# A transformer kernel on one core: input splits, square sums, a transfer and a modulation moved in the order of the engines

## The chip, the cores and the metric

The kernel runs on one core of a Trainium2 chip. The metric is the device time of one execution in microseconds (us); a lower time is better. Three runs of the kernel before took 2363.65 to 2364.48 us, with a median of 2364.28.

## The reference

All arithmetic is float32. There are 256 tokens of width 1024 and a second input, a context of 256 tokens. The first block has two layers: RMS norm, input projection, four kinds of attention, output projection, RMS norm, and a squared-ReLU network.

```python
        x = x + mixed @ w_out[layer]
        h2 = _rmsnorm(x, norm_mlp[layer])
        x = x + jnp.square(jax.nn.relu(h2 @ w_up[layer])) @ w_down[layer]
    return _rmsnorm(x, final_norm)
```

The second block works on tokens and context. Its first mixer is an mLSTM with four heads: queries and keys, a gated and decayed product of them, values, an output gate and an RMS norm of each head. Its last lines:

```python
        o = jax.nn.sigmoid(h_in @ w_og).reshape(Bq, T, M_HEADS, M_DV)
        hsum = o * s.transpose(0, 2, 1, 3).astype(h_in.dtype)
        return _head_rms_norm(hsum, norm_g) @ w_out
```

A convolved feed-forward network, a latent attention and a second feed-forward network follow.

## The kernel before, in words

Every activation lies in SBUF with features on the partitions: `xT` (the residual), `hT` (the modulated input of the second block) and an arena with everything else, reused by stage. A linear layer is a **group** of the stream plan: `("up", l, i)`, `("down", l)`, `("m_qk", h)`, `("m_og", h)` and so on. Its weights come from DRAM in slots of 128 x 2048 (1 MB) into `ring`, which has two places. It runs over **chunks** of 128 input features; `g.q0` is a group's first chunk and `g.s0` its first weight slot in the order of the whole program.

TensorE multiplies in the fp32r format with each operand split into a high and a low part, so each product is three matmuls (L757 where the activations move, L762 where the weights move). The high part is a copy made by ScalarE: `ws` from `ring` (L1236) and `xs` from the source (L1258 with a gain, L1260 without). The low part is the difference, made by VectorE (L1694, L1716, L1719). `ws` has room for two slots. `xs` has four cells of 256 columns: four chunks of 256 tokens, or two of 512. A copy waits until the chunk that held its place before has been multiplied.

ScalarE and VectorE each have the same three helpers: `weights_to(s)` splits slots up to s; `feed_to(q)` splits chunks up to q, and at the second and the last chunk of a slot also the next weight slot; `feed(g, more)` goes to the end of a group and `more` chunks beyond. Nothing is scheduled at run time: the order of each engine is the order of these calls and of the evictions between them, and an engine stands at each wait.

SyncE issues all large transfers. `load(w)` waits until the slot w - 1 has been split, then loads slot w. At the start the bias vectors (12 rows) are written to DRAM and read back as overlapping rows (`hankel`, `tz`), which VectorE reverses into the bias tables after `dma_bias`.

The results of TensorE go to eight PSUM banks, given out in a fixed order of tickets (`ticket_plan`): ticket n uses bank n % 8, so a product waits until the eviction of the ticket eight before it. In a mixer head the tickets are: 2 for the running maximum (`m_max`), 4 for `m_qk`, 4 for the scores (`m_QK`), 4 for the output gate (`m_og`), 1 for the denominator, 2 for its reciprocal, 4 for the product with the values (`m_PV`), 1 for the head's square sum (`m_rms`). The second quarter of `m_PV` so reuses the first bank of `m_og`, and chunk 0 of the next `m_qk` those of the last reciprocal and of `m_PV`.

**A mixer head.** TensorE: `m_max`, four chunks of `m_qk`, the square sum of the head before (L1089), the other twelve chunks, the scores (L1098), the output gate's eight chunks with denominator (L1109) and reciprocal (L1119) between them, then `m_PV` (L1127). ScalarE feeds `m_og` and chunk 0 of the next `m_qk`, evicts the gate by four sigmoids (L1516), loads the exp/ln table, and squares the head's 128 x 2048 result (L1519). VectorE multiplies the decays by the reciprocals (L2104), adds the two directions (L2109), feeds the gate's last chunk and chunk 0 of the next head, and multiplies `m_PV` by the gate (L2115). GpSimd adds the four squared tiles in two steps (L1672, L1674) for the first three heads; the fourth head's are summed by TensorE. At the next head VectorE continues with chunk 1, two memsets and chunks 2 and 3, then the exponents (L2060, L2067).

**Up and down.** Each up group's four bank pairs are evicted by VectorE (L1935, ReLU and scale) and squared by ScalarE (L1428) into `act`, the input of down. `relu` has two places, so the third eviction waits for the first square. At the last up group both engines first feed two chunks beyond it.

**The end of layer 1.** VectorE modulates the context half of `hT` (L1965, eight tiles), adds down's result to the residual (L1734), ScalarE squares (L1270), TensorE sums them in two steps (`group_sums` L867, `spread_sum` L877) with products of constants between them (`keep_warm`, L830) that nobody reads. ScalarE makes the root (L1294, L1296), and VectorE scales, modulates and feeds the first chunks of `m_up`.

## Time and profile before

| | us |
|---|---|
| median of 3 runs | 2364.28 |
| profiled execution, whole | 2365.65 |
| its span, first to last instruction | 2363.5 |
| TensorE busy with matmuls | 2255.5 (95%) |
| VectorE busy | 1354.2 (57%) |
| ScalarE busy | 1194.4 (51%) |
| GpSimd busy | 12.2 (1%) |

The mean granted clock of TensorE over the span is 0.995 of full speed. The span holds all stages in one stream, so a stage is read from its own stretch: layer 0 up to about 400 us, layer 1 to 774, the widening layer and the gates to 897, the values to 1082, the four mixer heads to 1460, then the rest. In a timeline row the first number is the start and the second the time from the first to the last instruction of the row; x4 is their count; in brackets stands how long the engine was idle before the row, and who released it. PE is TensorE, DVE VectorE, ACT ScalarE, POOL GpSimd, SPq the queue of SyncE.

### The profile page before, as it was taken

Reading aid. Unit: us, or ns where it says so; the run is one execution under the profiler, and the core shown is the slowest. Engines: PE = TensorE matmul, PEld = TensorE weight load, DVE = VectorE, ACT = ScalarE, POOL = GpSimd, SP = SyncE. Lnnn points to the kernel's source line nnn. Section 1 sums busy time; section 2 is a strip of 40 time slices with the busy share of each in tenths; the row PEclk is TensorE's granted clock in tenths of the full one; section 3 lists DMA queues with packets and bytes.
Section 4 is the critical chain, followed back from the end, with each engine's and each line's share of the span. In section 5 each row is a group of like instructions: output and inputs, shape, how many; then the busy total and the mean of one; then the engine's idle time right before and its main releaser. Section 6 shows DMA issues by size and latency. Waiting matters only on the chain.

```text
span 2363.5 us, 33820 instructions
## 1 busy us (share of the span) xinstructions
PE 2255.5 (95%) x13592; PEld 1859.8 (79%) x13592; DVE 1354.2 (57%) x2252; ACT 1194.4 (51%) x2020; POOL 12.2 (1%) x10
## 2 busy tenths in 40 slices
PE   8999999999999899999999999999999997899998
PEld 7759999957999777787676666867777876658998
DVE  5665655666665665445556555356565346446774
ACT  4556545555554563444344342256565335546764
POOL 0000000000000000000000000000000000000000
PEclk9999999999999999999999999999999999999999
DMA  7864544793445213222121121222222222204542
GB/s 296 324 251 143 183 174 179 281 361 125 175 165 185 85 69 107 89 89 90 53 89 54 72 72 47 96 72 89 90 89 98 99 89 73 106 19 156 184 163 106
DMA packets 45721, 312.31 MB, mean 132 GB/s; under 512 B 4951, under 2 KB 7255, under 8 KB 8580
## 3 DMA queue, kind: packets, MB, share of 16 engines
q1 hardware_dynamic: 45572, 310.20, 36.3%
q8 instruction: 108, 1.77, 0.3%
q14 instruction: 41, 0.34, 0.0%
HBM read 309.11 MB, written 1.07 MB: 131 GB/s over the span
## 4 chain that ended last, share of the span: by engine, by line
PE 80%; DVE 10%; ACT 7%; issue 2%; DMA 1%; ACTq 0%; SPq 0%; DVEq 0%
PE bank L757 56%; PE bank L762 8%; DVE ws L1694 3%; ACT ws L1236 2%; PE bank L966 2%; PE bank L1127 2%; DVE xs L1719 2%; PE bank L1027 1%; PE bank L1098 1%; PE bank L830 1%; PE bank L952 1%; PE bank L951 1%; PE bank L1008 1%; DVE arena L2104 1%; ACT xs L1260 1%
## 5 line engine op out<-in xcount | busy, mean ns | idle before, releaser
L757 PE MATMUL bank<-xs,ws 128*128 128x256 f32 (+1 forms) x9648 | 1570.0, 324 | 60.7 <-DVE xs L1719 48.9
L757 PEld LDWEIGHTS bank<-xs,ws 128*128 128x128 f32 x9648 | 1398.4, 191 | 234.0 <-DVE xs L1719 65.5
L1694 DVE TENSOR_TENSOR ws<-ring,ws 128x1024 fp32r<-128x1024 f32 x464 | 550.9, 1228 | 278.6 <-ACT ws L1236 278.4
L1236 ACT ACTIVATE ws<-ring 128x1024 fp32r<-128x1024 f32 x464 | 464.6, 1049 | 287.0 <-PE bank L757 279.2
L1719 DVE TENSOR_TENSOR xs<-arena,xs 128x512 fp32r<-128x512 f32 (+1 forms) x286 | 166.8, 599 | 305.6 <-ACT xs L1260 304.7
L1260 ACT ACTIVATE xs<-arena 128x512 fp32r<-128x512 f32 (+1 forms) x286 | 148.9, 538 | 338.1 <-PE bank L757 224.6
L762 PE MATMUL bank<-ws,xs 128*128 128x512 f32 (+1 forms) x1008 | 230.2, 388 | 6.3 <-ACT arena L1495 2.2
L1719 DVE TENSOR_TENSOR xs<-hT,xs 128x512 fp32r<-128x512 f32 (+1 forms) x216 | 133.0, 619 | 178.5 <-ACT xs L1260 178.5
L762 PEld LDWEIGHTS bank<-ws,xs 128*128 128x128 f32 x1008 | 188.5, 189 | 46.8 <-DVE xs L1719 3.2
L1260 ACT ACTIVATE xs<-hT 128x512 fp32r<-128x512 f32 (+1 forms) x216 | 122.8, 575 | 199.0 <-PE bank L757 190.3
L1716 DVE SCALAR_TENSOR_TENSOR xs<-xT,par,xs 128x256 fp32r<-128x256 f32 x112 | 51.1, 479 | 14.5 <-ACT xs L1258 11.9
L1258 ACT ACTIVATE xs<-xT,par 128x256 fp32r<-128x256 f32 x112 | 51.8, 495 | 6.8 <-DVE xT L1734 6.8
L830 PE MATMUL bank<-con 128*128 128x256 f32 x204 | 50.2, 401 | 2.2 <-DVE arena L2217 2.2
L966 PE MATMUL bank<-arena,cs 128*32 128x256 f32 x768 | 51.4, 385 | 0.0
L830 PEld LDWEIGHTS bank<-con 128*128 128x128 f32 x204 | 40.8, 202 | 11.7 <-issue 6.0
L1270 ACT ACTIVATE arena<-xT 128x512 f32<-128x512 f32 (+1 forms) x52 | 28.4, 563 | 39.5 <-DVE xT L2143 26.4
L1449 ACT ACTIVATE arena<-bank,par 128x512 f32<-128x512 f32 (+1 forms) x60 | 41.8, 697 | 11.1 <-PE bank L757 11.1
L1868 DVE SCALAR_TENSOR_TENSOR arena<-bank,arena 128x384 f32<-128x384 f32 x40 | 22.3, 557 | 41.2 <-PE bank L952 41.2
L1375 ACT ACTIVATE arena<-arena 128x128 f32<-128x128 f32 x40 | 16.1, 402 | 58.4 <-DVE arena L1871 58.4
L1127 PE MATMUL bank<-arena 128*128 128x512 f32 (+1 forms) x128 | 41.9, 485 | 0.0
L1957 DVE SCALAR_TENSOR_TENSOR arena<-arena,par 128x510 f32<-128x510 f32 (+1 forms) x60 | 38.8, 647 | 3.3 <-ACT arena L1466 3.3
L1959 DVE SCALAR_TENSOR_TENSOR arena<-arena,par 128x510 f32<-128x510 f32 (+1 forms) x60 | 39.2, 653 | 2.1
(263 smaller groups left out, 1479.0 us busy)
## 6 DMA issues: line engine op xcount, KB each, us to landing
ring<-in_stream SPq DMA_DIRECT2D x233, 1024.0 KB, 4.8
arena<-in_side SPq DMA_DIRECT2D x56, 1024.0 KB, 7.0
arena<-bias_vectors SPq DMA_DIRECT2D x1, 1536.0 KB, 10.4
hT<-in_tokens SPq DMA_DIRECT2D x1, 1024.0 KB, 6.3
arena<-in_tokens SPq DMA_DIRECT2D x1, 1024.0 KB, 13.5
out<-arena SPq DMA_DIRECT2D x2, 512.0 KB, 3.1
arena<-in_params SPq DMA_DIRECT2D x1, 918.0 KB, 9.7
arena<-bias_vectors SPq DMA_DIRECT2D x1, 706.0 KB, 11.8
```

The lines of the kernel that those rows point to most:

```text
L757: ins = mm(ps(n, c, c + g.T), a[wi][:, p * P:(p + 1) * P], x[xi], start=first, stop=last)
L762: ins = mm(ps(n, 0, width), x[xi][:, (p // nh) * P:(p // nh + 1) * P], a[wi][:, (p % nh) * 512:(p % nh) * 512 + width], start=first, stop= ...
L830: mm(ps(n, at, at + cols), ones, con[:, 0:cols], start=True, stop=True)
L966: ins = mm(bank[n % BANKS][c:c + 32, 0:T], cs[:, k, 2 * ADA_B - 2 - 2 * u:2 * ADA_B + 30 - 2 * u], wd[:, k, :], start=(u == 0 and k < 4), ...
L1127: ins = mm(ps(n, T_AT[st_], T2), mv[:, st_, h * T2 + e * P:h * T2 + (e + 1) * P], mP[:, 0, OFF[st_]:OFF[st_] + T2 - T_AT[st_]], start=(st_ ...
L1236: do(ws[:, i % 2, 0, c], ring[:, w % R, c], ACT.Copy).then_inc(w_high, 1)
L1258: do(split_x(q, 0), source(g, k), ACT.Identity, scale=par_at(g.gain, k)).then_inc(x_high, 1)
L1260: do(split_x(q, 0), source(g, k), ACT.Copy).then_inc(x_high, 1)
L1449: return do(dst, ps(n, 0, cols), ACT.Identity, scale=w[:, 1:2], bias=b)
L1694: ins = v.tensor_tensor(ws[:, i % 2, 1, c], ring[:, w % R, c], ws[:, i % 2, 0, c].bitcast(F32), ALU.subtract)
L1716: stt(split_x(q, 1), source(g, k), par_at(g.gain, k), split_x(q, 0).bitcast(F32), ALU.mult, ALU.subtract).then_inc(x_done, 1)
L1719: v.tensor_tensor(split_x(q, 1), source(g, k), split_x(q, 0).bitcast(F32), ALU.subtract).then_inc(x_done, 1)
```

## The change

Seven edits in the order of the engines; the arithmetic is the same except for the engine that adds the squares.

- Bias rows: SyncE issues the two reads of the bias vectors behind three ring loads, not four.
- Last root: three more constant products before the last `group_sums`; the eight context modulations stand between the chunk splits of layer 1's down, at chunks 10 to 17, not behind them.
- Last up group, in both layers: ScalarE and VectorE feed one chunk beyond it, not two. ScalarE splits down's chunk 1 and the weight slot behind it after two of the four squares, VectorE after the four evictions.
- Head loop, output gate: VectorE splits the gate's last chunk before the add of the two directions.
- Head loop, next head: both engines split chunks 0 and 1 of the next `m_qk` before the evictions of the gate (ScalarE) and of `m_PV` (VectorE). The weight slot behind them, which chunk 1 used to bring with it, comes after the sigmoids on ScalarE and after the first product on VectorE (`ahead=False`).
- Squares: GpSimd's two adds move to VectorE, behind the two memsets; its block goes.
- `mod_at` and `modulate_part` are defined earlier.

```diff
@@ -667,12 +667,13 @@
             sp.wait_ge(bank_free[N("bias") % BANKS], N("bias") // BANKS + 1)
             sp.dma_start(scratch, relu[0:12, 0, :]).then_inc(dma_bv, 16)
-            for i in range(4):
+            for i in range(3):
                 load(R + i)
             sp.wait_ge(dma_bv, 16)
             hnd = scratch.tensor
             sp.dma_start(hankel, bass.AP(tensor=hnd, offset=128, ap=[[1, P], [512, 12], [1, T]])).then_inc(dma_bias, 16)
             sp.dma_start(tz, bass.AP(tensor=hnd, offset=4 * 512, ap=[[1, P], [512, 4], [1, 353]])).then_inc(dma_bias, 16)
+            load(R + 3)
@@ -1044,6 +1045,7 @@
                     linear(G("up", l, i))
                 linear(G("down", l))
+            keep_warm(N(("m_up", 0)), T, T, 3)
             group_sums(2 * DEPTH)
@@ -1236,7 +1238,7 @@
                     fed["w"] += 1
-            def feed_to(q_):
+            def feed_to(q_, ahead=True):
@@ -1259,7 +1261,7 @@
                         do(split_x(q, 0), source(g, k), ACT.Copy).then_inc(x_high, 1)
                     fed["q"] += 1
-                    if (k % g.kc == 1 or k == g.K - 1) and follows(s_):
+                    if ahead and (k % g.kc == 1 or k == g.K - 1) and follows(s_):
                         weights_to(s_ + 1)
@@ -1421,8 +1423,10 @@
                 for i in range(4):
                     g = G("up", l, i)
-                    feed(g, 1 if i < 3 else 2)
+                    feed(g, 1)
                     for j in range(4):
+                        if i == 3 and j == 2:
+                            feed_to(G("down", l).q0 + 1)
                         n = N(g.name) + j
@@ -1509,11 +1513,15 @@
                     act_.wait_ge(bank_full[n % BANKS], n // BANKS + 1)
                     (do(mqk[:, j, :], ps(n), ACT.Copy, scale=1.0 if j < 2 else 1.0 / 16)).then_inc(bank_free[n % BANKS], 1)
-                feed(G("m_og", h), int(h < 3))
+                feed(G("m_og", h))
+                if h < MH - 1:
+                    feed_to(G("m_qk", h + 1).q0 + 1, False)
                 for j in range(4):
                     n = N(("m_og", h), j)
                     act_.wait_ge(bank_full[n % BANKS], n // BANKS + 1)
                     do(og[:, j, :], ps(n), ACT.Sigmoid).then_inc(bank_free[n % BANKS], 1)
+                if h < MH - 1:
+                    weights_to(G("m_qk", h + 1).s0 + 1)
                 exp_ln_tables()
@@ -1664,16 +1672,6 @@
-        @block.gpsimd
-        def _(pool):
-
-            for h in range(1, MH):
-                pool.wait_ge(sq_ready, SQ_HEADS + h)
-                nc.gpsimd.tensor_tensor(mqk[:, 0:2, :], mqk[:, 0:2, :], mqk[:, 2:4, :], ALU.add).then_inc(pool_own, 1)
-                pool.wait_ge(pool_own, h)
-                nc.gpsimd.tensor_tensor(mqk[:, 0, :], mqk[:, 0, :], mqk[:, 1, :], ALU.add).then_inc(pair_ready, 1)
-
-
         @block.vector
...
@@ -1719,7 +1717,7 @@
                                         ALU.subtract).then_inc(x_done, 1)
                     fed["q"] += 1
-                    if (k % g.kc == 1 or k == g.K - 1) and follows(s_):
+                    if ahead and (k % g.kc == 1 or k == g.K - 1) and follows(s_):
                         weights_to(s_ + 1)
@@ -1734,6 +1732,16 @@
                     if j == 1 and g:
                         feed_to(g.q0)
+
+            def mod_at(l, part, k, seg):
+
+                c = 2 * (KD * part + k) + 1 - seg
+                return mod[:, l, c:c + 1]
+
+            def modulate_part(k, seg):
+
+                t = slice(seg * T, seg * T + T)
+                return v.tensor_scalar(hT[:, k, t], xT[:, k, t], mod_at(0, 1, k, seg), mod_at(0, 0, k, seg), ALU.mult, ALU.add)
@@ -1924,7 +1932,7 @@
                 for i in range(4):
                     g = G("up", l, i)
-                    feed(g, 1 if i < 3 else 2)
+                    feed(g, 1)
                     if i == 0:
@@ -1934,14 +1942,14 @@
                         stt(relu[:, j % 2, :].rearrange("p (a b) -> p a b", a=2), pair_of(n), 0.0, scaled_by(stat), ALU.max, ALU.mult
                             ).then_inc(bank_free[n % BANKS], 1)
+                if l == DEPTH - 1:
+
+                    for k in range(KD):
+                        feed_to(G("down", l).q0 + 10 + k)
+                        modulate_part(k, 0)
                 feed(G("down", l))
                 if l < DEPTH - 1:
                     residual(("down", l), G("proj", l + 1, 0))
-
-            def mod_at(l, part, k, seg):
-
-                c = 2 * (KD * part + k) + 1 - seg
-                return mod[:, l, c:c + 1]
@@ -1959,13 +1967,6 @@
-            def modulate_part(k, seg):
-
-                t = slice(seg * T, seg * T + T)
-                return v.tensor_scalar(hT[:, k, t], xT[:, k, t], mod_at(0, 1, k, seg), mod_at(0, 0, k, seg), ALU.mult, ALU.add)
-
-            for k in range(KD):
-                modulate_part(k, 0)
             residual(("down", DEPTH - 1), None)
@@ -2047,6 +2048,12 @@
                 v.memset(mP[:, 0, 512:640], 0.0)
                 v.memset(mP[:, 0, 1280:1408], 0.0).then_inc(dve_own, 1)
+                if h:
+
+                    dve.wait_ge(sq_ready, SQ_HEADS + h)
+                    v.tensor_tensor(mqk[:, 0:2, :], mqk[:, 0:2, :], mqk[:, 2:4, :], ALU.add).then_inc(pair_own, 1)
+                    dve.wait_ge(pair_own, h)
+                    v.tensor_tensor(mqk[:, 0, :], mqk[:, 0, :], mqk[:, 1, :], ALU.add).then_inc(pair_ready, 1)
                 dve.wait_ge(dve_own, own(dve_own))
@@ -2105,10 +2112,15 @@
                     if z == 0:
                         feed_to(gates.q0 + 6)
+                feed_to(gates.q0 + 7)
                 dve.wait_ge(bank_free[n % BANKS], n // BANKS + 1)
                 v.tensor_tensor(mP[:, 0, :], mP[:, 0, :], mP[:, 1, :], ALU.add).then_inc(W_ready, 1)
-                feed(gates, int(h < MH - 1))
+                feed(gates)
+                if h < MH - 1:
+                    feed_to(G("m_qk", h + 1).q0 + 1, False)
                 for e in range(4):
+                    if e == 1 and h < MH - 1:
+                        weights_to(G("m_qk", h + 1).s0 + 1)
                     n = N(("m_PV", h), e)
```

## Rows read from the trace of the kernel before

**Rows 1.** The page, part 4: the chain that ended last, shares of the span by engine

```profile
PE 80%; DVE 10%; ACT 7%; issue 2%; DMA 1%; ACTq 0%; SPq 0%; DVEq 0%
```

**Rows 2.** Waits of TensorE, 1080 to 1475 us: us in total, times, longest

```profile
PE bank L757 <- DVE xs L1719: 16.1, 14, 1.7
```

**Rows 3.** Timeline, end of mixer head 0: start us, us, engine, line, operation

```profile
1157.58 1.76 DVE L2109 TENSOR_TENSOR arena<-arena 128x1536 f32<-128x1536 f32 x1
...
1159.45 1.28 ACT L1516 ACT_TABLE_LOAD   x1
...
1159.99 3.06 PE L757 MATMUL bank<-xs,ws 128*128 128x512 f32 x12 [1.23 <-DVE xs L1719]
1161.01 2.68 ACT L1516 ACTIVATE arena<-bank 128x512 f32<-128x512 f32 x4 [0.28 <-PE bank L757]
...
1162.89 10.48 PE L1127 MATMUL bank<-arena 128*128 128x512 f32 x32
...
1174.13 1.92 ACT L1519 ACTIVATE arena<-arena 128x2048 f32<-128x2048 f32 x1 [9.15 <-DVE arena L2115]
...
1176.13 2.38 POOL L1672 TENSOR_TENSOR arena<-arena 128x1024 f32<-128x1024 f32 x1 [1175.67 <-ACT arena L1519]
...
1176.60 2.45 DVE L1719 TENSOR_TENSOR xs<-arena,xs 128x512 fp32r<-128x512 f32 x1 [2.50 <-ACT xs L1260]
...
1179.11 3.03 PE L757 MATMUL bank<-xs,ws 128*128 128x512 f32 x12 [1.74 <-DVE xs L1719]
...
1182.72 1.29 DVE L1719 TENSOR_TENSOR xs<-arena,xs 128x512 fp32r<-128x512 f32 x2
...
1183.47 5.74 PE L757 MATMUL bank<-xs,ws 128*128 128x512 f32 x24 [1.33 <-DVE xs L1719]
```

**Rows 4.** Timeline, last up group to down, layer 0, then layer 1

```profile
304.44 1.28 DVE L1935 SCALAR_TENSOR_TENSOR arena<-bank,stat 128x512 f32<-128x512 f32 x2
305.16 1.23 ACT L1428 ACTIVATE arena<-arena 128x512 f32<-128x512 f32 x2 [2.08 <-DVE arena L1935]
...
308.82 21.39 PE L757 MATMUL bank<-xs,ws 128*128 128x256 f32 x164 [2.10 <-DVE xs L1719]
...
685.42 14.79 PE L757 MATMUL bank<-xs,ws 128*128 128x256 f32 x109 [2.10 <-DVE xs L1719]
```

**Rows 5.** Timeline, end of layer 1's down and last root

```profile
759.81 13.72 PE L757 MATMUL bank<-xs,ws 128*128 128x256 f32 x113
...
771.24 2.67 DVE L1965 TENSOR_SCALAR hT<-xT,mod 128x256 f32<-128x256 f32 x8
773.83 2.47 DVE L1734 TENSOR_TENSOR xT<-xT,bank 128x512 f32<-128x512 f32 x4
...
777.01 0.64 PE L867 MATMUL bank<-arena,con 128*32 128x256 f32 x8 [0.47 <-ACT arena L1270]
777.58 1.91 PE L830 MATMUL bank<-con 128*128 128x256 f32 x4
```

**Rows 6.** Timeline of the start

```profile
23.83 2.36 DVE L1694 TENSOR_TENSOR ws<-ring,ws 128x1024 fp32r<-128x1024 f32 x2 [3.75 <-ACT ws L1236]
...
42.05 2.01 ACT L1236 ACTIVATE ws<-ring 128x1024 fp32r<-128x1024 f32 x2 [3.23 <-PE bank L757]
...
46.40 20.42 PE L757 MATMUL bank<-xs,ws 128*128 128x256 f32 x168 [1.57 <-DVE xs L1716]
```

**Rows 7.** Timeline of ScalarE at a table load in the widening layer

```profile
815.01 1.28 ACT L1470 ACT_TABLE_LOAD   x1
816.30 0.63 ACT L1470 ACTIVATE arena<-arena 128x512 f32<-128x512 f32 x1
```

**Rows 8.** Busy time by engine and granted clock (PEclk, before the DMA share)

```profile
779.28:780.13 0.85, 0.85 (x3) 0.67 (x2) 0.00 (x0) 0.00 (x0) 0.00 (x0) 0.50 0.00 0
```

**Rows 9.** Chain that ended last, at the start: start us, us

```profile
34.01 11.83 DMA arena<-bias_vectors
```

**Rows 10.** The page, part 6: issues, KB each, median us to landing

```profile
ring<-in_stream SPq DMA_DIRECT2D x233, 1024.0 KB, 4.8
```

More of the change, by code:

```diff
@@ L581, in build @@
         gate_exp = sem("gate_exp_ready")
-        pair_ready, pool_own = sem("head_squares_added"), sem("pool_own")
+        pair_ready, pair_own = sem("head_squares_added"), sem("half_squares_added")
         cond_exp = sem("condition_exp_ready")
@@ L1696, in weights_to, with feed_to @@
                     fed["w"] += 1
-            def feed_to(q_):
+            def feed_to(q_, ahead=True):
                 while fed["q"] <= q_:
```

## The prediction

> **What bounds the kernel now.** I read the shares of the chain that ended last first: TensorE holds 80% of it, VectorE and ScalarE 17% [rows 1]. So an edit is worth what it takes out of TensorE's idle gaps, and nothing more. Then I read TensorE's waits stage by stage, and for each gap the timeline around it: who released it, and what that engine was doing instead. In the mixer's head loop TensorE waits 16.1 us in 14 gaps for a VectorE input split [rows 2]. In head 0 three gaps stand out: 1.23 us before the last chunk of the output gate, then 1.74 and 1.33 us before chunks 1 and 2 of the next head's query-key group [rows 3]. Heads 1 and 2 repeat these three, and head 3 has the first only: 4 x 1.23 + 3 x (1.74 + 1.33) = 14.1 of the 16.1. Outside the head loop the change touches a 2.10 us gap where the last up group gives way to down, once in each layer [rows 4], a seam at the end of layer 1 where TensorE has finished and others work [rows 5], and one gap of 1.57 us at the start [rows 6].
>
> **Output gate, last chunk.** VectorE splits this chunk's input only after its 1.76 us add L2109, and ScalarE had made the high half long before. The added feed to chunk 7 puts the 0.7 us split ahead of the add. The input is then ready at about 1158.3 and the matmuls follow chunk 6 without the 1.23 us. The add ends at 1160.0, and the value products that need it begin at 1161.8 [rows 3]. Hidden, then. Four heads: 4 x 1.23 = 4.9 us.
>
> **Next head's chunks ahead.** Chunk 1's input buffer is free once the output gate's last matmul has ended (T, now 1163.05). ScalarE makes its copy only behind the squares, near 1176.0, and VectorE's split then takes 2.45 us against 0.65 for each of two later ones, because GpSimd's adds run from 1176.13. Chunk 2 is late because its split, at 1182.72, is queued on VectorE behind this one and the weight split [rows 3]. After the change chunks 0 and 1 are split before the gate's evictions, and the second weight slot behind the sigmoids (ScalarE) and behind the first product (VectorE). TensorE then has two chunks, 5.8 us, to run, and only chunks 2 and 3 are to be split meanwhile. Both gaps go: 3.07 us for each of three transitions, 9.2 us.
>
> What is queued behind the new waits: ScalarE now waits for T before the four sigmoids, which had begun 2.0 us ahead of T. The copy (0.63), the table load (1.28) and one sigmoid (2.68 / 4 = 0.67) end at T + 2.6. The second quarter of the value products writes the bank that this first sigmoid frees, and it is due at T + 10.48 / 4 = T + 2.6 [rows 3]. It is a tie. With the hand-off it costs 0 to 0.3 us, and I take 0.2, three times: -0.6 us. The later sigmoids come every 0.67 us against 2.6 us of products, so they are in time. On VectorE the second, third and fourth products wait behind the weight split. ScalarE gives its halves at about T + 5.7 and T + 6.7, so the split ends near T + 8 and the second and third products near T + 9.5. The banks they free are wanted by the next head's chunk 0 at T + 11.7. The fourth product waits for TensorE anyway. Free, with 2 us of cover; without it each late us would be paid three times.
>
> **Squares on VectorE.** Two instructions more for each of three heads. 1.76 us for 1536 columns [rows 3] gives 1.2 for 1024 and 0.6 for 512. VectorE waits for the 1.92 us square first, so it stands from the fourth product to the end of the square and then works 1.8 us. Behind it are the split of chunk 2, whose high half is ready only when chunk 0 has ended, 4 us after the square began, and the decay exponents. The sum is wanted after chunk 3, some 8 us later. Cost nothing; if that cover were gone, 1.8 us a head. Taking GpSimd away also gives VectorE back at least 2.45 - 0.65 = 1.8 us, counted already in the gaps.
>
> Heads together: 4.9 + 9.2 - 0.6 = **13.5 us**. The other two us of waits (before chunk 6 of each group) stay.
>
> **Table load.** In the trace a load of 1.28 us is followed by its own function 0.01 us after it ends [rows 7]. The Trainium skill ("ScalarE: Activation LUTs", What ACT_TABLE_LOAD costs) adds a drain of about 1.38 us to each switch. The trace disagrees and decides the forecast. By that page, an estimate, the tie above would become 1.4 us late a transition, and the sum 4 us smaller.
>
> **Last up group to down, both layers.** Now both engines do chunks 0 and 1 of down and the weight slot behind them before the evictions. VectorE is in that slot's split until its first eviction at 304.44, the squares follow, and chunk 2 comes 2.10 us late [rows 4]. Down's chunks 0 and 1 (2.9 us each) end at 308.82 - 2.10 = 306.7, so up ends at 301.0, and in its last chunk the four banks fill 0.7 us apart from 298.9. After: only chunk 0 ahead, and VectorE can evict from about 299.1. Two squares are done at 301.1, then come ScalarE's copy of chunk 1 and the slot (2.0 us), to 303.5, two more squares to 304.8, and chunks 2 and 3. VectorE ends the slot at 305.0 and chunk 2 at 305.5. TensorE wants chunk 1 at 303.9 (split 302.3) and chunk 2 at 306.7. The gap closes with 1.2 us to spare: 2 x 2.10 = **4.2 us**.
>
> **Last root.** Down's matmuls end at 759.81 + 13.72 = 773.53. VectorE ran the eight context modulations (2.67 us) right before the four residual adds, whose first bank was full at 771.4 [rows 5]. Woven into down they cost VectorE 0.33 us in each of eight chunks, 0.7 us in a slot of 5.8 us in which the weights take it 2.36 [rows 6] and the two half-width inputs under 1.3: hidden. The last residual add then ends at about 774.2, its square at 774.85, and the group sums at 775.5, against 777.01 + 0.64 = 777.65. The three added warm products (six instructions) run meanwhile. Four such took 1.91 us at a granted clock of about 0.5 [rows 5, 8], so six take 1.4 us at full clock, until 774.9. Both square pairs then queue behind them and the sums end at about 776.0: 1.7 us gained, 2.1 without that queue. What follows on TensorE (the two warm products, then the spread) ran at a granted clock of 0.50, that is at the 1.2 GHz level, after TensorE had done almost nothing for 3.5 us [rows 5, 8]. With the warm products in the hole I expect the 2.4 GHz level, which saves half of 1.91 us and about 0.3 on the spread, 1.2 us. Sum 2.9, bounds 1.7 and 3.3: **2.9 us**.
>
> **Bias rows.** The transfers were issued behind the fourth ring load, at 34.0, which waits for the fourth weight split. VectorE waited for their landing 11.83 us later, and TensorE 1.57 us behind it [rows 6, 9]. Behind the third load they are issued when the split that begins at 23.83 ends, so at 26.6, and land near 38.9, well before the split that TensorE wanted at 46.40 - 1.57 = 44.8. The whole gap goes, **1.6 us**. The fourth ring load now queues behind them: issued at 33.2, it lands at 38.0 if undisturbed, or 4.8 us after them [rows 10], at 43.7. ScalarE takes it at 42.05 [rows 6], and the split made of it has some 1.1 us to spare, so the cost is 0 to 0.6 us. I take 0.
>
> **Sum.** 13.5 + 4.2 + 2.9 + 1.6 = 22.2 us. The profiled execution took 2365.65 (span 2363.5 and 2.15 around it), so it becomes 2343.5. The median of the runs lies 1.37 below that execution, which gives **2342.1 us**, 0.94% faster. The forecast's own range is 2339.5 to 2345.
>
> **Rivals.** First, the sigmoids: the head-of-line wait on ScalarE costs more than the tie, because a drain comes with the load or the weight slot comes late on VectorE. Rows 7 speak against it; for it is that nothing in the trace shows a copy, a load and a sigmoid with TensorE waiting for them. At 1.4 us more in each of three transitions it gives 2346.3. Second, the clock falls at the last root in spite of the warm products, and the first loads meet the bias rows: 1.2 and 0.6 less, 2343.9, inside the forecast's range. Third, the change does only part of what it says: the two chunks are split ahead but a new late item takes their place (chunk 2 behind the square adds, or chunk 1 of down behind the slot), so that 9.2 or 4.2 us become half or none. It gives 2346 to 2351, say 2348.5; the cover of 1.2 to 2 us speaks against. Fourth, slower: the clock. TensorE is granted the 1.2 GHz level after a hole like that of rows 5 and 8. If the new order left it there after the last root, each us of work due at full clock would take one more. It would have to last for over 22.2 us of such work to make the kernel slower, and over 27 us to be slower by 0.2%; at 35 us it gives 2377. Against it: the holes become shorter, not longer.
>
> **Chances.** Forecast (with the second rival) 0.74, sigmoids 0.11, partial 0.11, clock 0.02, and 0.02 for a gain that another wait takes whole. About 0.2%, 4.7 us, is what a measurement of this kernel can tell from no change: faster 0.95, same 0.03, slower 0.02. The range that leaves out no more than 2 in 10 runs from 2338.5 (all bounds favourable, and some of the two us before chunk 6 too) to 2348.5.
>
> **What would show it.** In the profile after: no wait of TensorE before chunk 7 of the output gate and before chunks 1 and 2 of a query-key group, and waits for VectorE in the head loop of about 2 us; a wait of some 0.2 us between the first two quarters of the value products, released by the sigmoid (over 1 us there is the first rival); splits of 0.7 us everywhere; 24 matmuls of down's first chunks running on without a gap; a granted clock of 1.00 through the last root, with the first Ln some 2.9 us sooner after down's end; the bias rows landed by 39. A new gap at chunk 2 or 3, or at the fourth ring slot, would make the prediction wrong.

## The result and the profile after

The kernel after took 2336.43 us in the median of four runs (2334.79 to 2337.46). The kernel before took 2364.38 on the same chip (2363.65 to 2368.02). The ratio is 0.988, interval 0.987 to 0.990. By that interval the gain lies between 24 and 31 us, so the difference from the forecast is more than noise. The forecast of 2342.1 had the direction and the order of size. The gain was 27.95 us where it said 22.2, and the time lies 2.1 us below the low end of the range. The profiled execution took 2337.17 us, its span 2335.3, against 2365.65 and 2363.5 before. Of the 24 executions of the kernel before that the first four experiments are compared with, one took 2723.78 us at a mean granted clock of 0.77 and is left out below.

I read the profile after in the same order as the one before. The chain that ended last (page, part 4), the answer to rows 1:

```profile
PE 83%; DVE 8%; ACT 7%; issue 2%; DMA 0%; ACTq 0%; DVEq 0%; SPq 0%
```

VectorE lost two points of the chain and TensorE gained three. The waits of TensorE from 1070 to 1460 us (waiting line, what for: us in total, times, longest), the answer to rows 2:

```profile
PE bank L758 <- DVE xs L1717: 2.0, 4, 0.5
```

From 16.1 us in 14 gaps to 2.0 in 4: the ten gaps named in the prediction are gone, and the ones before the gate's chunk 6 are left. The end of head 0 in the timeline of the kernel after (start us, us, engine, line, operation; in brackets the idle time before), the answer to rows 3:

```profile
1140.46 5.76 PE L758 MATMUL bank<-xs,ws 128*128 128x512 f32 x24 [0.49 <-DVE xs L1717]
...
1142.80 1.74 DVE L2117 TENSOR_TENSOR arena<-arena 128x1536 f32<-128x1536 f32 x1
...
1146.06 10.80 PE L1129 MATMUL bank<-arena 128*128 128x512 f32 x32
...
1146.90 1.28 ACT L1522 ACT_TABLE_LOAD   x1
...
1148.20 2.06 ACT L1522 ACTIVATE arena<-bank 128x512 f32<-128x512 f32 x4
...
1157.84 11.19 PE L758 MATMUL bank<-xs,ws 128*128 128x512 f32 x48
1159.57 1.23 DVE L2054 TENSOR_TENSOR arena<-arena 128x1024 f32<-128x1024 f32 x1 [1.70 <-ACT arena L1527]
1160.83 0.69 DVE L2056 TENSOR_TENSOR arena<-arena 128x512 f32<-128x512 f32 x1
```

The gate's last two chunks are one run of 24 matmuls, and the next head's chunks 0 to 3 one of 48. The product with the values takes 10.80 us where it took 10.48: that is the tie with the first sigmoid, which frees the bank of the product's second quarter just when it is due, 0.32 us where the prediction had 0.2. The seam of layer 0 (where the last up group gives way to down) and the start of the last root, the answers to rows 4 and 5:

```profile
291.82 20.44 PE L758 MATMUL bank<-xs,ws 128*128 128x256 f32 x169
...
762.72 1.46 PE L831 MATMUL bank<-con 128*128 128x256 f32 x6
764.11 1.07 PE L868 MATMUL bank<-arena,con 128*32 128x256 f32 x16
765.11 1.13 PE L831 MATMUL bank<-con 128*128 128x256 f32 x4
```

169 matmuls run through the seam without a gap. At the root both square sums follow the six new warm products in one piece, and the four constant products behind them take 1.13 us against 1.91. At the start (the answer to rows 6) the bias rows are issued at 25.55 and 26.02 us, and 126 matmuls run through the place of the 1.57 us gap:

```profile
25.55 0.43 SPq L674 DMA_DIRECT2D arena<-bias_vectors  x1
26.02 2.50 SPq L675 DMA_DIRECT2D arena<-bias_vectors  x1
...
34.91 15.36 PE L758 MATMUL bank<-xs,ws 128*128 128x256 f32 x126
```

So every named gap closed and no new one came, and yet the sum was 5.8 us short. To find where, I set the start of the same matmul side by side in the two traces, at the borders of the stages. The table gives how much earlier the kernel after is there, and what each stage added.

| border in the trace of before, us | earlier, us | of the stage | forecast |
|---|---|---|---|
| first transposes, 7.6 | 0.91 | 0.91 | 0 |
| layer 0, down chunk 0, 300.8 | 2.98 | 2.07 | 1.6 |
| layer 0, down chunk 2, 308.8 | 5.24 | 2.26 | 2.10 |
| layer 0, down chunk 4, 316.1 | 6.78 | 1.54 | 0 |
| layer 1, down chunk 2, 685.4 | 9.10 | 2.32, of it 2.26 at the seam | 2.10 |
| layer 1, down chunk 4, 692.7 | 10.65 | 1.55 | 0 |
| first matmul behind the last root, 783.8 | 13.66 | 3.01 | 2.9 |
| end of the values, 1082.4 | 15.29 | 1.63 | 0 |
| four heads, 1461.4 | 31.39 | 16.10 | 13.5 |
| last matmul, 2358.2 | 28.21 | -3.18 | 0 |

Three terms have no forecast at all: 1.5 us behind each seam, 1.63 in the values, and -3.18 behind the heads. The heads gave 2.6 more than forecast. The granted clock (PEclk, the number before the DMA share) explains the first kind. The kernel before, two stretches behind the gaps of rows 4 and one in the values:

```profile
304.00:308.80 4.80, 2.73 (x23) 2.53 (x23) 3.56 (x7) 3.42 (x7) 0.00 (x0) 1.00 0.64 218
310.00:313.50 3.50, 3.50 (x20) 3.50 (x19) 2.47 (x4) 0.96 (x3) 0.00 (x0) 0.52 0.16 23
686.00:689.00 3.00, 3.00 (x16) 3.00 (x16) 2.97 (x4) 1.55 (x3) 0.00 (x0) 0.50 0.00 0
...
952.00:955.00 3.00, 3.00 (x9) 2.33 (x8) 0.69 (x1) 0.27 (x1) 0.00 (x0) 0.50 0.66 279
```

The kernel after, which is 5.2 to 15.3 us ahead at these places: behind the first seam, behind the second and in the values. The last line is a place of its own behind the heads:

```profile
304.00:308.80 4.80, 4.80 (x42) 4.80 (x42) 3.03 (x4) 2.47 (x4) 0.00 (x0) 1.00 0.56 186
...
676.00:679.00 3.00, 3.00 (x28) 3.00 (x27) 1.33 (x2) 2.42 (x4) 0.00 (x0) 1.00 0.82 314
...
937.00:955.00 18.00, 18.00 (x79) 14.91 (x80) 6.43 (x8) 6.33 (x9) 0.00 (x0) 1.00 0.34 117
...
1955.00:1960.00 5.00, 5.00 (x26) 5.00 (x25) 0.56 (x3) 1.26 (x2) 0.00 (x0) 0.50 0.33 139
```

In three microseconds at the 1.2 GHz level 16 matmuls of 256 columns run, at the 2.4 GHz level 28. The forecast had looked at the clock in one place only, the last root.

### The profile page after: what moved, and what is told of

Same layout as the page of the kernel before. It is cut to its first block, busy times and chain, and to the rows that moved or that the text cites. A ratio compares the mean times of both kernels' runs of the same rounds, so it can differ in the third digit from the quotient of the medians.

```text
span 2335.3 us, 33830 instructions
## 1 busy us (share of the span) xinstructions
PE 2251.0 (96%) x13598; PEld 1859.4 (80%) x13598; DVE 1352.0 (58%) x2258; ACT 1193.7 (51%) x2020; POOL 0.2 (0%) x4
## 4 chain that ended last, share of the span: by engine, by line
PE 83%; DVE 8%; ACT 7%; issue 2%; DMA 0%; ACTq 0%; DVEq 0%; SPq 0%
PE bank L758 59%; PE bank L763 8%; DVE ws L1692 3%; ACT ws L1238 2%; PE bank L967 2%; PE bank L1129 1%; DVE xs L1717 1%; PE bank L1028 1%; PE bank L1100 1%; PE bank L953 1%; PE bank L831 1%; PE bank L952 1%; PE bank L1009 1%; PE bank L1191 1%; ACT xs L1262 1%
## 5 line engine op out<-in xcount | busy, mean ns | idle before, releaser
L1377 ACT ACTIVATE arena<-arena 128x128 f32<-128x128 f32 x40 | 16.1, 402 | 58.4 <-DVE arena L1879 58.4
```

## The experiments

The theory at this point had two parts. One: a gap as long as that of the seam is followed by a stretch at half clock, which costs some 1.5 us beside the gap and goes with it. Two: the rest of the difference (values, end) is a matter of the execution, not of the change. The rival: the edits themselves make the later matmuls faster, by other timing of the operands, and then the 1.5 us belong to the clock of no gap. Each edit was also taken alone, to measure each term of the sum.

**The seam alone.** The kernel before with this edit:

```diff
-                    feed(g, 1 if i < 3 else 2)
+                    feed(g, 1)
                     for j in range(4):
+                        if i == 3 and j == 2:
+                            feed_to(G("down", l).q0 + 1)
```

> The kernel before with the edit at the last up group alone (both layers). The sum of the prediction says 2 x 2.10 = 4.2 us less. Theory A, half-clock stretches: each 2.10 us gap is followed by a stretch of 3.41 us at a granted clock of 0.5 (the trace of before has them at 310.2 and 685.6 us, that of the changed kernel has neither), in which matmuls take twice their time, so each seam costs 2.10 + about 1.7 and this kernel is 7.6 us faster; the stretches at 310 and 685 are missing from its records. Theory B, the seam is worth its gap and the rest came from elsewhere: 4.2 us faster.

Measured: 2358.27 us in the median of ten runs, 2363.45 before, ratio 0.9983 (0.9972 to 0.9994). In the trace of this kernel the first seam brings 2.25 us by chunk 2 and 1.55 more by chunk 4, the second 2.24 and 1.56: as in the kernel after within 0.02. This kernel is 4.1 us ahead at the first seam and 7.9 at the second. At the same work the granted clock is 1.00 where it was 0.52 and 0.50:

```profile
306.00:309.40 3.40, 3.40 (x31) 3.40 (x30) 3.03 (x4) 1.64 (x4) 0.00 (x0) 1.00 0.29 116
678.90:682.40 3.50, 3.50 (x31) 3.50 (x31) 3.01 (x4) 1.50 (x3) 0.00 (x0) 1.00 0.33 122
```

In this pair of traces a seam is worth 3.8 us, not 2.10. This doesn't yet separate the clock from the gap.

**The gap filled, not closed.** The kernel before, with eight matmuls of constants in the gap that nobody reads. The order on ScalarE and VectorE is as before, so chunk 2 is as late as before:

```diff
-                linear(G("down", l))
+                linear(G("down", l), 0, 2)
+                keep_warm(N(("down", l)) + 4, T, T, 4)
+                linear(G("down", l), 2)
```

> The kernel before, order of splits unchanged, with four constant products nobody reads (eight instructions, about 1.8 us) on TensorE in the gap behind down's chunk 1, in both layers. The gap itself stays: chunk 2 comes as late as before. Theory A (half-clock stretch behind the gap): the clock stays at 1.00 and each seam gives back about 1.7 us, 3.4 us faster in all, with down's chunk 2 starting at the same time behind up as before. Theory B (only the gap costs): no gain, 0 +/- 0.5 us.

Measured, TensorE at the first seam and the clock behind it:

```profile
308.34 1.89 PE L830 MATMUL bank<-con 128*128 128x256 f32 x8
...
310.60 5.63 PE L757 MATMUL bank<-xs,ws 128*128 128x256 f32 x45 [0.37 <-DVE xs L1721]
...
311.90:315.40 3.50, 3.50 (x32) 3.50 (x31) 2.35 (x4) 0.84 (x3) 0.00 (x0) 1.00 0.23 42
```

Chunk 2 starts no earlier than without the products (0.00 and 0.01 us at the two seams), but chunk 4 is 1.48 and 1.49 us earlier. So the operands come when they came before and only the clock is another: the rival, an effect of the operands' timing, falls. The whole time shows none of it: 2362.37 in ten runs, ratio 1.0000 (0.9990 to 1.0009). In this trace a long stretch at half clock at 92 us took 3.2 us, and another at the last root 1.0. I can't show that it was so in all ten runs. The interval reaches 2.2 us to either side, so it would not show a gain of 1.6 us for both seams, the mean that follows below.

But is it the filled gap that held the clock, or would it have held anyway? The other experiments answer, since four of them leave both seams as they were. In the five traces with the gaps of rows 4 (the kernel before, the gate alone, the chunks ahead alone, the squares alone, the bias rows alone) the clock fell behind 5 of 10 seams: in layer 0 in that of before and of the bias rows, in layer 1 in that of before, of the gate and of the chunks ahead. In the eight traces in which the gap is filled or closed it fell behind none of 16. So the gap makes the fall possible, and does not bring it each time. A closed seam is worth 2.25 us in every trace, and 1.55 us more in those in which the clock would have fallen: by these ten seams half of them, 0.8 in the mean.

**The gate's last chunk alone.** The kernel before with `feed_to(gates.q0 + 7)` ahead of the add of the two directions.

> The kernel before with only the output gate's last chunk split ahead of VectorE's add (four heads). The prediction's term is 4 x 1.23 = 4.9 us. Theory A, a gap costs more than its idle time, because matmuls are pipelined and a stream that stops has to run in again: 1.5 us a head by the start of the value products in the changed kernel, 6.2 us. Theory B, the idle time is the price: 4.9 us.

Measured: 2356.63 us in seven runs, ratio 0.998 (0.9966 to 0.9994). In the trace of before (first fence) and in this one (second):

```profile
1155.74 3.02 PE L757 MATMUL bank<-xs,ws 128*128 128x512 f32 x12 [0.49 <-DVE xs L1719]
```

```profile
1155.00 5.73 PE L757 MATMUL bank<-xs,ws 128*128 128x512 f32 x24 [0.49 <-DVE xs L1719]
1160.57 10.48 PE L1127 MATMUL bank<-arena 128*128 128x512 f32 x32
```

From the start of chunk 6 to that of the products with the values it takes 1160.57 - 1155.00 = 5.57 us. Before, it was 1162.89 [rows 3] - 1155.74 = 7.15. The edit is worth 1.58 us in head 0 and 1.54, 1.53 and 1.54 in the others, 6.2 in all, where the idle time in the brackets is 1.23.

**The next head's chunks ahead, squares left on GpSimd.** The kernel before with these lines, and the same on VectorE with the weight slot behind the first product:

```diff
-                feed(G("m_og", h), int(h < 3))
+                feed(G("m_og", h))
+                if h < MH - 1:
+                    feed_to(G("m_qk", h + 1).q0 + 1, False)
...
+                if h < MH - 1:
+                    weights_to(G("m_qk", h + 1).s0 + 1)
```

> The kernel before with only the next head's chunks 0 and 1 split ahead and the weight slot behind the first product; GpSimd still adds the squares and the gate's last chunk is split as before. Prediction's term: 3 x 3.07 - 3 x 0.2 = 8.6 us. If gaps cost 0.3 us more than their idle time, 3 x (3.07 + 0.6) - 3 x 0.3 = 10.1 us. If GpSimd's adds (4 us from the end of the square, in which VectorE's two-input instructions stand still) still delay the split of chunk 2, a gap of up to 0.5 us stays before chunk 2 and the gain is up to 1.5 us smaller. A wait of 0.2 to 0.3 us appears between the first two quarters of the value products.

Measured: 2353.20 us in six runs, ratio 0.9962 (0.9949 to 0.9975). In the trace:

```profile
1160.31 10.80 PE L1127 MATMUL bank<-arena 128*128 128x512 f32 x32
...
1172.09 11.18 PE L757 MATMUL bank<-xs,ws 128*128 128x512 f32 x48
```

The tie costs 0.31 us, and each transition is a net 3.32 to 3.37 us shorter, with GpSimd still adding. The kernel after has 3.32 to 3.35, both by the starts of the product with the values and of the next head's scores. So with the chunks ahead it makes no difference which engine adds the squares.

**Squares on VectorE alone.** The kernel before with GpSimd's two adds behind the two memsets of VectorE.

> The kernel before with only the squares moved from GpSimd to VectorE; the next head's chunk 1 is still split behind them. Theory A, GpSimd's adds hold VectorE up: the split of chunk 1 takes 0.69 instead of 2.45 us, so the gap before chunk 1 (1.74 us) all but goes, and the one before chunk 2 (1.33) changes by what the square sums (1.9 us on VectorE, now ahead of chunk 2's split behind the weight slot) and the faster weight split (2.36 against 3.43) make together: about +0.8. Between chunk 0 and the scores 1.5 to 2.0 us a transition less. Theory B, the move alone is worth nothing, since VectorE only exchanges a stall for work: within 0.3 us a transition. The prediction gave the move no gain of its own.

Measured in one run, 2361.53 us against 2364.51. TensorE and VectorE at the first transition, and the clock before and behind the gap:

```profile
1167.18 6.00 PE L757 MATMUL bank<-xs,ws 128*128 128x512 f32 x24
...
1169.42 0.69 DVE L1709 TENSOR_TENSOR xs<-arena,xs 128x512 fp32r<-128x512 f32 x1 [2.50 <-ACT xs L1260]
...
1170.16 2.59 PEld L757 LDWEIGHTS bank<-xs,ws 128*128 128x128 f32 x12 [0.40 <-DVE xs L1709]
...
1172.93 1.16 DVE L2043 TENSOR_TENSOR arena<-arena 128x1024 f32<-128x1024 f32 x1
...
1175.47 7.36 PE L757 MATMUL bank<-xs,ws 128*128 128x512 f32 x24 [2.29 <-DVE xs L1709]
...
1168.00:1172.00 4.00, 4.00 (x18) 3.02 (x17) 2.32 (x3) 3.81 (x5) 0.00 (x0) 1.00 0.02 4
1177.00:1180.00 3.00, 3.00 (x8) 2.32 (x7) 0.85 (x3) 0.17 (x1) 0.00 (x0) 0.50 0.01 3
```

Neither theory had this. VectorE's split of chunk 1 is short again (0.69 us) and the gap before it shrinks to 0.40, but the adds now stand ahead of chunk 2, whose gap grows to 2.29. The shown idle falls by 3.07 - 2.69 = 0.4 us, and by the starts of the matmuls chunk 2 follows chunk 0 after 8.29 us instead of 9.11. Then the clock falls: 24 matmuls take 7.36 us against 5.74. Each transition became 0.73 to 0.80 us slower, in all three heads. So the order alone gains 0.8 us, and the half clock behind the longer gap costs 1.6, in three of three transitions. The whole time does not show the loss: in this trace the clock held at layer 1's seam, at the last root and in the values, where it fell in that of before, and that is worth 4.2 us. With the chunks ahead the move neither gains nor loses.

**The bias rows alone.** The kernel before with three ring loads ahead of the bias rows and the fourth behind.

> The kernel before with only the bias rows' transfers behind the third ring load. Prediction's term: 1.57 us, between the root's transposes and the compression products. If a gap costs 0.3 us more than its idle time, 1.85 us. If the fourth ring load, now behind the bias rows, comes late, less, down to nothing, and a wait of ScalarE for it shows at 42 us.

Measured in one run, 2360.82 us against 2364.51. From the first root (1.17 us earlier than before) to the start of attention's first matmuls (2.99) it brings 1.82 us, the kernel after 1.84. The forecast was 1.6, the shown idle 1.57. The gap is gone, and no wait came at the fourth slot:

```profile
34.78 25.44 PE L758 MATMUL bank<-xs,ws 128*128 128x256 f32 x210
```

**The last root without its warm products.** The kernel after without `keep_warm(N(("m_up", 0)), T, T, 3)`.

> The changed kernel without the three added products of constants before the last root's group sums. The prediction's working: the group sums then end 0.4 us sooner, but with TensorE idle for about 1.5 us the granted clock may fall as in the kernel before, which costs 1.2 us: from down's end to the widening layer's first matmul 0.4 us less if the clock stays at 1.00, up to 0.8 us more if it falls to 0.5.

**The last root without the weave.** The kernel after with the eight modulations behind down again, as in the kernel before, and not woven between its chunk splits.

> The changed kernel with the eight context modulations put back behind down, the three warm products kept. The weave is worth 1.7 to 2.1 us by the prediction (the residual adds start at 773.8 again, counted on the clock of the kernel before); the warm products alone then keep the clock at best, 1.2 us of the seam's 3.0. So from down's end to the widening layer's first matmul about 1.8 us more than in the changed kernel, and 1.2 us less than in the kernel before if the clock stays at 1.00; equal to the kernel before if a half-clock stretch falls there again.

Measured in one run each (the two kernels just named), TensorE from down's end on. First without the warm products, then without the weave:

```profile
766.53 0.64 PE L868 MATMUL bank<-arena,con 128*32 128x256 f32 x8
767.87 0.64 PE L868 MATMUL bank<-arena,con 128*32 128x256 f32 x8 [0.70 <-ACT arena L1271]
768.44 1.13 PE L831 MATMUL bank<-con 128*128 128x256 f32 x4
```

```profile
765.75 1.46 PE L831 MATMUL bank<-con 128*128 128x256 f32 x6
768.30 0.64 PE L868 MATMUL bank<-arena,con 128*32 128x256 f32 x8 [1.08 <-ACT arena L1272]
769.40 0.64 PE L868 MATMUL bank<-arena,con 128*32 128x256 f32 x8 [0.46 <-ACT arena L1272]
769.97 1.13 PE L831 MATMUL bank<-con 128*128 128x256 f32 x4
```

Without the warm products the stage is 3.24 us shorter than before, so they cost 0.2 us instead of bringing 1.2. Without the weave 1.18 us are left of the 3.01. The clock stayed at full speed in both, as the 1.13 us rows show (1.91 in rows 5): with the weave alone as with the warm products alone. Whole times: 2339.71 and 2342.49 against 2364.51. Here too one trace isn't enough for the clock, and the others help: with the root as before it fell in 6 of 7, with one or both of the two edits in none of 6. In the seventh of the first kind (the squares alone) it held, and the stage was 1.19 us shorter for that alone. So the clock is worth 1.2 us as forecast, and the warm products alone bring just this and no more. But the weave brings it as well: their gains don't add, and the three warm products could have been left out.

**The kernel after once more, and two versions of it.** The same kernel ran again beside two that go at the gaps left over.

> The changed kernel once more, unaltered. Its trace is the second of the same program: what differs between the two is not the program's. The transposes' start (6.69 us against 7.60 in the first trace of before) should vary with the landing of the first tokens. The half-clock stretches behind 1950 us (1953.8, 2001.6, 2022.0, 2240.5 in the first) should fall elsewhere or in another number if they depend on when the chip looks, and in the same places if the program alone sets them. Up to 1950 us both traces should agree within 0.3 us once started, with no half-clock stretch at the two seams and at the last root. Time against the kernel before: 0.988.

Measured: 2337.18 us in four runs (2334.07 to 2340.23), before 2367.05, ratio 0.988 (0.986 to 0.990). The profiled spans differ by 0.2 us, 2335.1 and 2335.3, but not in the same places. One stretch of the same program, the trace shown above first and then this one:

```profile
462.00:464.00 2.00, 1.01 (x9) 0.69 (x8) 0.91 (x5) 1.75 (x6) 0.00 (x0) 1.00 1.02 430
467.00:471.00 4.00, 4.00 (x45) 2.52 (x37) 3.14 (x8) 2.72 (x6) 0.00 (x0) 1.00 1.01 418
```

```profile
462.00:464.00 2.00, 1.01 (x9) 0.69 (x8) 1.11 (x7) 1.55 (x6) 0.00 (x0) 1.00 0.98 414
467.00:471.00 4.00, 4.00 (x27) 2.73 (x27) 2.39 (x5) 2.55 (x5) 0.00 (x0) 0.50 1.01 426
```

With the same work ahead of it, the second execution ran at the 1.2 GHz level at 467 us and lost 3.1 us there. I had expected the two to agree up to 1950 us. It also lacked the 1.63 us of the values, since its clock fell at 940 us. Behind the heads it then gained 1.59 on the trace of before, where the first had lost 3.18.

The next version moves two more splits. VectorE splits the gate's chunk 6 ahead of the first multiplication by the reciprocals, and ScalarE copies chunk 6 of the query-key group ahead of the exponentials:

```diff
-                    feed_to(g.q0 + 5 + 5 * z)
+                    feed_to(g.q0 + 6 + 4 * z)
...
+                    if z == 0:
+                        feed_to(gates.q0 + 6)
                     ...
-                    if z == 0:
-                        feed_to(gates.q0 + 6)
```

> The changed kernel with the two gaps that are left in each head closed: chunk 6 of the output gate is split ahead of VectorE's first multiplication by the reciprocals (0.49 us of idle before it), and chunk 6 of the query-key group is copied by ScalarE ahead of the decay exponentials (0.53 us before chunk 6). With 0.3 us of run-in for each gap: 4 x 0.8 + 3 or 4 x 0.8 = 5.6 to 6.4 us less than the changed kernel. By idle time alone 4.1 us. If the split moved ahead delays what follows it on VectorE (the multiplications, so the value products), less.

Measured: 2334.74 us in four runs, ratio 0.987 (0.9853 to 0.9886).

```profile
1141.87 5.73 PE L758 MATMUL bank<-xs,ws 128*128 128x512 f32 x24
1147.83 3.01 PE L758 MATMUL bank<-xs,ws 128*128 128x512 f32 x12 [0.23 <-DVE xs L1717]
```

The 0.49 us gap before chunk 6 is gone, but chunk 7 got one of 0.23, since VectorE's order only changed places. Each head gains 0.3 us there and 0.4 at the other copy. From the end of the values to that of the heads it gains 18.6 us on the kernel before, where the kernel after on the same chip gains 16.2. I had expected more than twice that difference, 5.6 to 6.4 us. The last version adds a load of the sigmoid's table between the copies of the next head's chunks 0 and 1:

```diff
-                feed(G("m_og", h))
+                feed(G("m_og", h), int(h < MH - 1))
+                act_.preload_act_table_set("sigmoid_and_others")
```

> The same, with the sigmoid table loaded between the copies of the next head's chunks 0 and 1, so that the first sigmoid no longer waits for the load behind the gate's last matmul. The changed kernel has a wait of 0.31 us between the first two quarters of the value products in heads 0 to 2, as its trace shows by the start of the next head's maximum. It should go: 0.9 us less than with the two gaps alone. Whole time about 2329 to 2331 us.

Measured: 2334.74 us in four runs, ratio 0.987 (0.9854 to 0.9887).

```profile
1143.29 1.28 ACT L1517 ACT_TABLE_LOAD   x1
...
1145.91 0.63 ACT L1262 ACTIVATE xs<-arena 128x512 fp32r<-128x512 f32 x1 [1.33 <-PE bank L758]
...
1146.45 2.04 ACT L1523 ACTIVATE arena<-bank 128x512 f32<-128x512 f32 x4
```

The product with the values from its first to its last matmul, in the same trace:

```profile
1145.71 10.48 PE L1129 MATMUL bank<-arena 128*128 128x512 f32 x32
```

The load now runs while ScalarE waits for TensorE, and the tie is gone: the product with the values is back at its old length, 0.00 us against the 0.31 of the other. In the trace the heads gain 19.5 us on before, 3.3 more than the kernel after, and the profiled span is 2330.6. The whole time expected was 2329 to 2331, so that missed. In the medians it isn't told from the version before it, and both lie 2.4 us below the kernel after, inside the 6 us over which the kernel after's own four executions spread (2334.07 to 2340.23). That they beat it is likely by the traces and not shown by the times.

## Why the prediction was right and wrong

**Right: which gaps go, and that none comes.** All ten in the heads, both at the seams, the one at the start. The covers that I named held (the add of the gate, the weight slot behind the first product, the fourth ring load), and so did the tie of the first sigmoid: 0.31 to 0.32 us against 0 to 0.3, taken as 0.2.

**The first rival** didn't come. The load of the sigmoid's table began 0.01 us behind the copy ahead of it and ended at 1148.18, and the function began at 1148.20. The Trainium skill ("ScalarE: Activation LUTs", What ACT_TABLE_LOAD costs) adds a drain of about 1.38 us to a switch. These rows show 0.02 us between load and function, and the tie paid for no more than it, so the trace doesn't agree.

**Wrong, the first term: a seam at 2.10 us.** I took the idle time in brackets as the price of a gap. The gap was followed by a stretch at half clock, in both layers, which the view of busy time and granted clock of before would have shown, had I asked for it behind the gap (0.52 and 0.50). It was worth 1.55 us a seam, 3.1 in this pair of traces, and the filled gap showed that it is the clock. Over many executions I take it at half, since the clock fell behind 5 of 10 such gaps. So the term of 4.2 us measured 7.6 in this pair. My prediction used the mechanism, but only at the last root.

**Wrong, the second term: the idle time itself.** A gap costs more than its brackets say, wherever an edit was taken alone and no clock moved: 1.23 shown and 1.53 to 1.58 paid (gate), 3.07 shown and 3.36 + 0.31 = 3.67 paid (two gaps of a transition), 1.57 shown and 1.82 paid (bias rows), 2.10 shown and 2.25 paid (seam). That is 0.15 to 0.35 us a gap. It hides in the record of the last matmul before a gap and in the first ones behind it: 12 matmuls alone stand as 3.01 us, while 48 in one run take 11.19, or 2.80 for 12. The record of one such matmul is 0.39 us long where the next starts 0.23 us after it, and the idle time is counted only from the record's end. In the heads this is 4 x 0.32 for the gate and 3 x 0.6 for the transitions, 3.1, less 3 x 0.11 for the tie, which was put at 0.2: 2.8, where the heads gave 2.6 beyond 13.5. With 0.3 at the seams and 0.2 at the bias rows it is 3.1 us in all.

**Right size, wrong reason: the last root.** 3.01 us, forecast 2.9. The clock's 1.2 us are there, but I credited them to the warm products, and in the kernel without these the clock held too and the root was 0.2 us shorter. The weave and the shorter hole are worth 1.8, forecast 1.7.

**Squares on VectorE** were put at nothing, and are at nothing in this order; but the 1.8 us of VectorE that the prediction counted among the gaps did not help close one, since with the chunks ahead and the adds on GpSimd each transition is as short. That edit could have been left out too.

**By chance.** The clock also fell at places that no edit touches. By the table the first transposes were 0.91 us earlier, but in the traces of all eleven experiments, none of which changes anything ahead of them, they were earlier too, by 0.63 to 1.25. So it is that one execution of before that began late. The 1.63 us of the values and the -3.18 behind the heads come from half-clock stretches that lie elsewhere in each execution. The three sum to -0.6 us. So the account of the profiled pair is 22.2 + 3.1 (clock at the seams) + 3.1 (the gaps' own size, tie included) + 0.1 (root) - 0.6 = 27.9, against 28.2 measured. For the medians, with half of the clock at the seams and no chance, it is 22.2 + 1.6 + 3.1 + 0.1 = 27.0, against 27.95, which is inside the interval of 24 to 31. That where the clock falls behind the heads is no matter of the program is shown by the kernel after run twice. Why a given gap is followed by half clock in one execution and not in the next stays open.

**The range** was too narrow below. Its low end took all the bounds of single gaps, but not that the shown idle of each could be too small, and nothing for the clock's scatter: the kernel before took 2358.25 to 2367.32 us in 23 executions on one chip.

## What to carry to other kernels

Price a gap of TensorE by the start of the matmuls on both sides of it against the same matmuls in an unbroken run, and not by the idle time alone; then read the granted clock right behind it, since half clock there can belong to the gap and go with it. It need not come in each execution, so take it from several traces. Of two measures against the same fall of the clock count one. Before moving work from a slow engine to the one that feeds TensorE, look at which input it will stand ahead of: here the same move was free with two chunks in store, and without them it lost 0.8 us a head to the half clock behind a longer gap.

## What the runs showed of the hardware

- The clock fell behind holes as short as 2.10 us (both layers of before) and 2.29 us (squares alone, in three of three transitions), from 1.00 to 0.50, which cost about 1.55 us at a seam and 1.62 behind the gap of 2.29. Of the seams' gaps of 2.10 us it did so behind 5 of 10, and behind the gaps of 1.23, 1.33 and 1.74 us of rows 3 in none of the heads. From these counts no threshold follows.
- The same program had its half-clock stretches at different places in two executions, with a cost of 1.6 to 3.2 us each. The spans came out equal by sum only.
- Four constant products of 256 columns that took 1.91 us at 0.50 took 1.13 at 1.00, and 24 matmuls of 512 columns 7.36 and 5.74.
- While GpSimd adds, a VectorE subtraction of 128 x 512 took 2.45 us, and 0.69 with the adds on VectorE itself, where the two adds take 1.23 and 0.69 us against GpSimd's 2.38 for the larger.
